# Where the delta rule's second preparation stands among the products of its levels

## The reference

```python
diff = gc[..., :, None] - gc[..., None, :]
decay = jnp.where(incl, jnp.exp(jnp.where(incl, diff, 0.0)), 0.0)
kb = kc * bc[..., None]
lhs = jnp.where(strict, jnp.einsum('nbhid,nbhjd->nbhij', kb, kc) * decay, 0.0) + jnp.eye(C, dtype=f32)
u = lax.linalg.triangular_solve(lhs, vc * bc[..., None], left_side=True, lower=True, unit_diagonal=True)
w = lax.linalg.triangular_solve(lhs, kb * jnp.exp(gc)[..., None], left_side=True, lower=True, unit_diagonal=True)
...
def step(state, xs):
    u_n, w_n, qk_n, qd_n, kd_n, gl_n = xs
    v_new = u_n - jnp.einsum('bhck,bhkv->bhcv', w_n, state)
    o_n = jnp.einsum('bhck,bhkv->bhcv', qd_n, state) + jnp.einsum('bhij,bhjv->bhiv', qk_n, v_new)
    state = state * gl_n[..., None, None] + jnp.einsum('bhck,bhcv->bhkv', kd_n, v_new)
    return state, o_n
```

## Time and profile before

| | us |
|---|---|
| median of 3 runs | 4107.07 |
| lowest, highest | 4103.67, 4107.86 |
| the profiled execution, its own time | 4095.71 |
| its span in the trace | 4093.9 |
| TensorE busy | 3633.7 (89%) |
| VectorE busy | 1768.6 (43%) |
| ScalarE busy | 1217.7 (30%) |
| GpSimd busy | 437.7 (11%) |

### The profile page before, as it was taken

The page is one execution under the profiler, slowest core; times in us unless marked ns, Lnnn a source line. Parts: engine busy times, 40 slices in busy tenths (PEclk is TensorE's granted clock), DMA queues, the critical chain, the costliest instruction groups (busy, mean ns, idle before and its releaser), DMA issues. The chain is left out here.

```text
span 4093.9 us, 49349 instructions
## 1 busy us (share of the span) xinstructions
PE 3633.7 (89%) x19466; PEld 2763.6 (68%) x19466; DVE 1768.6 (43%) x2376; ACT 1217.7 (30%) x1703; POOL 437.7 (11%) x422
## 2 busy tenths in 40 slices
PE   7999898888999699989979699977999797869997
PEld 6878564666877478767738488755787575347876
DVE  5532354545532365323555455223332356643322
ACT  3221433233221332223332322224322233233221
POOL 0000112520001000010034100011000200330001
PEclk9999898999999899999989899988999899879998
DMA  4332110013331134212200133212222122012221
GB/s 152 139 115 82 62 62 23 3 42 113 138 110 55 63 139 147 96 61 73 66 7 4 47 139 140 99 42 70 93 97 95 59 74 63 15 47 87 92 98 56
DMA packets 88124, 324.02 MB, mean 79 GB/s; under 512 B 12648, under 2 KB 14696, under 8 KB 87536
## 3 DMA queue, kind: packets, MB, share of 16 engines
q1 hardware_dynamic: 87920, 321.21, 23.3%
HBM read 319.06 MB, written 2.12 MB: 78 GB/s over the span
## 5 line engine op out<-in xcount | busy, mean ns | idle before, releaser
L214 DVE TENSOR_TENSOR w_low<-w_raw,w_high 128x1024 fp32r<-128x1024 f32 (+2 forms) x496 | 632.0, 1276 | 1497.4 <-ACT w_high L209 1497.0
L209 ACT ACTIVATE w_high<-w_raw 128x1024 fp32r<-128x1024 f32 (+2 forms) x496 | 543.6, 1098 | 1450.7 <-PE ffa_in_ps L228 265.5
L226 PE MATMUL ffa_in_ps<-ffa_x_high,w_high 128*128 128x512 f32 x704 | 281.7, 400 | 39.4 <-DVE ffa_x_low L271 39.4
L226 PE MATMUL f_in_ps<-b_f_x,w_high 128*128 128x512 f32 x704 | 282.8, 402 | 22.6 <-DVE b_f_x L359 21.5
L226 PE MATMUL ffb_in_ps<-ffb_x_high,w_high 128*128 128x512 f32 x704 | 281.6, 400 | 23.5 <-DVE ffb_x_low L271 23.5
L227 PE MATMUL ffa_in_ps<-ffa_x_low,w_high 128*128 128x512 f32 x704 | 280.4, 398 | 0.0
L228 PE MATMUL f_in_ps<-b_f_x,w_low 128*128 128x512 f32 x704 | 280.3, 398 | 0.0
L227 PE MATMUL f_in_ps<-b_f_x,w_high 128*128 128x512 f32 x704 | 280.3, 398 | 0.0
L227 PE MATMUL ffb_in_ps<-ffb_x_low,w_high 128*128 128x512 f32 x704 | 279.9, 398 | 0.0
L228 PE MATMUL ffa_in_ps<-ffa_x_high,w_low 128*128 128x512 f32 x704 | 279.6, 397 | 0.0
L228 PE MATMUL ffb_in_ps<-ffb_x_high,w_low 128*128 128x512 f32 x704 | 279.2, 397 | 0.0
(11 more groups left out here) (492 smaller groups left out, 6792.2 us busy)
## 6 DMA issues: line engine op xcount, KB each, us to landing
w_raw<-in_ffa_in SPq DMA_DIRECT2D x88, 512.0 KB, 5.1
w_raw<-in_ffb_in SPq DMA_DIRECT2D x88, 512.0 KB, 4.5
w_raw<-in_ffn_in SPq DMA_DIRECT2D x88, 512.0 KB, 3.3
w_raw<-in_mix_in SPq DMA_DIRECT2D x80, 512.0 KB, 3.5
w_raw<-in_ffa_out SPq DMA_DIRECT2D x32, 704.0 KB, 4.0
w_raw<-in_ffb_out SPq DMA_DIRECT2D x32, 704.0 KB, 4.1
w_raw<-in_ffn_out SPq DMA_DIRECT2D x32, 704.0 KB, 4.1
ffa_in_ada_raw<-in_w_ada SPq DMA_DIRECT2D x36, 512.0 KB, 3.5
```

What stands on the lines that cost most here:

```text
L209: act.activation(self.high[:, half, :kt * P], self.raw[:, slot, :kt * P], ACT.Copy).then_inc(self.rounded, 1)
L214: dve.tensor_tensor(self.low[:, half, :kt * P], self.raw[:, slot, :kt * P], self.high[:, half, :kt * P].bitcast(F32), ALU.subtract).then_i ...
L226: pe.matmul(out, w_high, x_high[:, k0 + k, :], start=start and k == 0, stop=False)
```

## The change

In `order`, the ten steps of the second preparation are yielded straight after the ten of the first and in the same order among themselves, before any step of the levels. The list `beside` is empty for the first group. Nothing else in the kernel differs; no instruction is added, removed or altered.

```diff
@@ -1130,11 +1130,12 @@
         before = [(step, c) for step in ("exps", "gram", "keys", "values", "fade") for c in range(2)]
         for step, c in before:
             yield step, c, 0
+        for step, c in before:
+            yield step, c + 2, 0
         for group in range(GC // 2):
             pairs = (2 * group, 2 * group + 1)
-            if group == 0:
-                beside = [[(step, c + 2, 0)] for step, c in before]
-            else:
+            beside = []
+            if group:
                 beside = [[(step, c - 2, n) for c in pairs]
                           for step, n in (*(("step", n) for n in range(2, N_CHUNKS - 1)), ("early", 0), ("late", 0), ("out", 0))]
             beside = iter(beside)
@@ -1144,8 +1145,6 @@
                 for step in ("y", "z"):
                     for c in pairs:
                         yield step, c, lv
-                        if group == 0:
-                            yield from next(beside, ())
                     if group:
                         yield from next(beside, ())
             for rest in beside:
```

## The result

| | kernel before | changed kernel |
|---|---|---|
| median, ten runs each | 4105.9 | 4114.6 |
| lowest to highest | 4093.7 to 4109.1 | 4110.3 to 4121.1 |
| ratio, 95% interval | | 1.0027, 1.0016 to 1.0037 |
| profiled execution, span | 4093.9 | 4112.7 |

The changed kernel is slower: by the ratio 11 us, with an interval from 6.6 to 15.2 us. That is 0.27% of the time: small, but outside the noise. The forecast was 12.4 us more and a time of 4119.5. On a second chip the same kernel had a ratio of 1.0035 (1.0021 to 1.0048), 14 us.

The account below looks back on a forecast made before the run. The stretch was taken as bounded by TensorE's products, its first 10 us by a chain through VectorE and GpSimd. 16.5 + 31.1 - 41.4 = +6.2 us a layer, +12.4 on the 4107.07 median: 4119.5 us, range 4113 to 4128.

Parts of the forecast that it names:

- The second preparation standing alone: Ten steps of pairs two and three before the eye products: 14.7 us at high clock, 16.5 with low clock from keys.
- The four named hand-overs: Waits in the second preparation: exps of pair three starts at 2.3 us, gram two 4.1, gram three 6.8, keys 9.5.
- The levels without it: First group's eye products to wu without preparation steps between: 3.95 + 6.6 + 16.8 + 3.75 = 31.1 us.
- The sum of +6.2 us a layer: Second preparation plus bare levels minus today's stretch: 16.5 + 31.1 - 41.4 us a layer, +12.4 us in all.
- the 3 us allowed: Spread between runs, taken off the high-clock case to set the forecast range's lower end: 3 us.
- high-clock rival: Granted clock stays high in the second preparation: +8.8 us in all, 4115.9 us; chance 0.18.
- Everything after wu is as before: Sign for the changed kernel's timeline: the stage behind the wu product keeps its time; 59.03 us follows the levels before.
- I am wrong if the levels take more than 32, or if the clock falls in the levels: Sign against the forecast, in the levels after the moved preparation: over 32 us, or a fall of the granted clock there.
- the nearest whole stretch: Check on the 14.7 us: the first preparation, the same ten steps on other banks, took 14.57 us.
- The low stretch in the levels of before: Low clock in the eye products and level one of the kernel before: costs about 1.6 us, already within the 41.37.
- The worth of the fillers: Preparation products between the levels' products: 7.4 us, from two exps of 1.05, two grams of 0.9, six transpose groups of 0.59.
- its row: Trace evidence against the skill's rule: from 743 to 752 us, mostly transposes before 747.60, the granted clock stayed at 1.00.

Follow-up runs that it names:

- second trace of before: Kernel before, unchanged, traced again: 54.4 and 52.5 us from the second group's eye products to the last output product; eye products to wu 40.1 us in layer one.
- second trace of the changed kernel: Changed kernel run again unaltered, against the kernel before on the same chip: ratio 1.0035 (1.0021 to 1.0048); stage start to wu 62.06 and 63.10 us.

## Why the prediction was right

The second preparation standing alone was put at 16.5 us, 14.7 of it chain and 1.8 low clock; it is 16.12 and 16.22, and with the clock held up 14.84, so the low clock costs 1.3 here where 1.8 was put. The four named hand-overs are there one for one: exps of pair 3 at 2.4 us (2.3), gram two at 4.2 (4.1), gram three at 6.9 (6.8), keys at 9.6 (9.5); at the high clock the eye products follow the keys after 5.2 us (5.2). The levels without it were put at 31.1 us and are 31.38 and 31.25; the second y product comes 1.96 us after the first, as estimated. The sum of +6.2 us a layer is +6.1, with some luck: the preparation came out 0.3 us short and the levels 0.2 long.

The clock was forecast from keys on, and fell there. It is not where the loss comes from. With the clock at 1.00 the second preparation and the levels take 46.0 us in the changed order and 40.1 in the order of before, 5.9 more a layer. The bare levels take 31.2, so beside them the second preparation costs 8.9 us; alone it costs 14.84, and with other banks 11.68. The hand-overs of the two banks are therefore 3.2 of the 5.9 us (2.7 of it reach wu, as the levels of that variant lost 0.5 to the low clock). The other 2.7 are what the ten steps still take longer alone than beside the levels; that these are the lists of GpSimd and VectorE is read from one timeline, and no run tests it.

What was off:
- The total. 4119.5 was forecast and 4114.6 measured. The difference between the kernels was 12.4 against 11 (by ratio; 8.7 by medians), and the 10 runs of before and the 3 shown have medians 1.2 us apart. It lies inside the noise of the clock, which was larger than the 3 us allowed. The time is 1.6 us above the range's lower end and closer to the high-clock rival's 4115.9 than to the forecast. So the time does not choose between these two; the granted clock in the trace does.
- "Everything after wu is as before" failed in the profiled execution: 62.06 and 61.90 us instead of 58.18. These 7.6 us come on top of the 12.5 us up to wu; 1.3 us less outside the stage make it the 18.8 us between the two spans. The second trace of before has 62.30 us there in layer one and 60.17 in layer two, so the change is not needed for it. The step that failed is taking one execution's rest of the stage as fixed. Whether the change makes the low clock there more likely, no run shows: all four layers of the changed kernel have it, and two of four of before.
- "I am wrong if the levels take more than 32, or if the clock falls in the levels" came true in the second trace of the changed kernel (32.14 and 32.72 us, the clock at 0.50 for 3.4 us), with a shorter preparation beside it. The sum held all the same within 0.1 us in layer one and was 1.1 us higher in layer two. The sign was too strict: where the clock falls moves between executions.
- The check against "the nearest whole stretch" was luck. The 14.57 us of the first preparation were run at a granted clock of 0.67; the same steps on the same banks at 1.00 take 11.68 us in the variant with other banks. The 14.7 us came out of the chain, not out of this likeness.
- The low stretch in the levels of before was put at 1.6 us and is 1.2 (41.4 beside 40.1).
- The worth of the fillers, 7.4 us with 0.59 for a group of transposes. In the levels such a group costs 0.72 to 0.76, so 8.3 us. The forecast was spared this, as it took the 41.37 whole, but the variant with half the steps in front missed by it.
- The Trainium skill ("TensorE: Matmul & The Clock Gate", Part 4: PE-mode transpose) says that transposes do not bring the full clock. The prediction was right not to build on it, but its row was not enough: from 743 to 752 us the clock was high already. The first trace of the changed kernel looks like the rule, with 5.90 of 6.51 us busy and a clock of 0.51. Its second trace does not agree with the rule: the clock rose to 1.00 at 758.5 us, after 3.4 us in which TensorE was busy for 2.87 us with nothing but transposes. Why the low stretch lasts 3.4 us in one layer and 6.8 in the other three with the same work, no run shows.

## What to carry to other kernels

A preparation put between the products of another chain costs little more than its own products, here 8.9 us for 8.3; standing alone it costs its round trips, here 14.8. Before moving a block, follow its own chain of waits through shared banks and price that, not its busy time. Where it must stand alone, give it other banks; and look for the places where the bounding engine idles, and put single steps just there: two exps beside the eye products took 1.3 us off a layer, and 1.2 more where the clock had fallen, while moving all ten steps had added 5.9. And compare stretches at the same granted clock: two traces of one kernel differ here by up to 4 us in the rest of one stage.

## What the runs showed of the hardware

- The granted clock fell not only after idle time but while TensorE worked in crumbs: in the last chunk steps it has 0.46 us of work and 0.19 us of waiting in turn, and in 14 of 22 layers the clock fell to 0.50 in them or behind them, which lengthens this part by 1.6 to 2.8 us. Where it falls differs from one execution to the next of the same kernel.
- Products that nobody reads held the clock at 1.00 and shortened the chain: 16.1 to 14.8 us with 16 matmul instructions in each of three gaps; 15.1 us in both layers with 8 in each of five, where 14 of 22 layers without them had 16.1 to 17.3.
- Four float32 128 x 128 transposes between groups of 64 x 64 products cost 0.72 to 0.76 us, and 0.59 from their start to the next product's.
- The granted clock came back from 0.50 to 1.00 while TensorE ran nothing but such transposes (second trace of the changed kernel, at 758.5 us in layer one and at 2181.9 in layer two).
